# A decoder layer in float32 on one Trainium2 core: the first six projection units summed over feature blocks in six PSUM banks, their modulation fetched in matching column steps, and router logits laid out in token rows

## The chip, the core and the metric

The kernel runs on one core of a Trainium2 chip. A core has TensorE (PE; its weight loads are shown apart as PEld), VectorE (DVE), ScalarE (ACT), GpSimd (POOL), and SyncE (SP), which here only starts transfers (DMAs). The metric is device microseconds of one execution of the whole kernel. Lower is better.

## What is computed

One decoder layer for 256 tokens of width 1024, all in float32, cut to what matters here:

```python
sh1, sc1, gt1, sh2, sc2, gt2 = jnp.split(silu(c) @ w_ada + b_ada, 6)
h = rmsnorm(x, norm1) * (1.0 + sc1) + sh1                 # 256 x 1024
proj = h @ w_in                                           # q, k, v | mLSTM qk, v, o, i/f | two gates
y_a = diff_attention(q, k, v, lam)                        # 4 heads, causal, ALiBi
y_m = mlstm(silu(causal_conv(ml_qk)), ml_v, i_f)          # 4 heads
x = x + gt1 * ((sigmoid(g_a) * (y_a @ w_br_a) + sigmoid(g_m) * (y_m @ w_br_m)) @ w_out)
h2 = rmsnorm(x, norm2) * (1.0 + sc2) + sh2
x = x + gt2 * hier_moe(h2)      # 4 groups of 8 experts: best group, two experts in it, all 32 weights read
return rmsnorm(x, norm_f)
```

## The kernel before, in words

**Units.** SP streams all weights through a ring of eight slots, in units of 1 MB. The order is the list UNITS (line 54). The six 1024-column parts of `w_ada` take four units each (`ada0` to `ada5`; a unit is two of the eight feature blocks by 1024 columns). A projection unit ("dense") is all eight feature blocks by 256 columns of `w_in`. Before a unit is requested, SP waits until the job that read the same slot eight units earlier is done (line 336). SP stands in that wait with everything that is listed after it.

**Splits.** Every dense product is made of three fp32r products, so that float32 precision is kept. ACT rounds a dense unit into `hi` (`split(d)`, lines 420 to 426, one of three buffers). POOL then subtracts it from the unit, in pieces of 512 columns, and leaves the low part (line 391). PE multiplies hi by hi, low by hi and hi by low (`product`, line 1238): 24 matmuls of 256 columns for each half of a unit. The modulated input `h` is kept in the same two parts, `hT_hi` and `hT_lo`.

**Banks.** PE writes into eight PSUM banks. The list JOBS (line 94) gives every result a bank, in turn: job n uses bank n mod 8. `take(job)` makes PE wait until the job eight places earlier has been read out. `cols` and `ada2` are eight places apart, and so share a bank; DVE reads `cols` out at line 882.

**The stage around the change.** PE computes `ada0` and `ada1` (the shift and scale of the first norm) as their units land. It transposes the normalised input (`xT0` to `xT3`). DVE and ACT apply the modulation out of PSUM, and only then do the products start: `if` (the input and forget gates of the mLSTM), four q/k units `qk0` to `qk3`, `ada3`, two v units `v0` and `v1`. Then come the attention scores of all four heads (`s0` to `s7`), the units `ml0`, `ml1`, then `ada4`, `ml2`, `ml3`; then `cols` and `Mb` (decay terms of the mLSTM), `mv0`, `mv1`, `rb` (router bias) and `ada2`. Further projections, the branches and the output follow, and then the router and the MoE loop.

**Orders written by hand.** Each engine runs its instructions strictly in the order of its code. ACT has, in this order: small DMA issues, the sum of squares of x, a wait for those DMAs (`bc_in`, line 435), the modulation, splits 0 to 2, then for each of `qk0` to `qk3` a copy out of PSUM and one split, two more splits, and then for each head the exponentials, a copy of `ml{h}` and a split. DVE has the gate arithmetic (lines 777 to 806: `ifT`, then scans), `scores(h)` (lines 808 to 820), `combine(h)` (822 to 832), `conv(i)`, and then the column forms of the modulation and the copy of `cols`.

**Router and MoE.** The router logits are computed transposed (36 rows by 256 tokens, line 1486) into the bank `lgT`, copied by DVE (line 1030), transposed back by PE (line 1498) into `lg`, and read by DVE (line 1032). The MoE loop reads 96 units of expert weights. Sixteen are requested before the loop starts, into slots as they come free (lines 360 to 364); each later one waits until the loop has used up a unit (line 356, semaphore `used`).

## Time and profile before

| | |
|---|---|
| median of 3 runs | 506.74 us (506.46 to 506.91) |
| the profiled execution | 506.75 us |
| its span in the profile | 505.0 us |
| PE busy | 426.5 us (84%) |
| DVE busy | 159.5 us (32%) |
| ACT busy | 173.7 us (34%) |
| POOL busy | 157.3 us (31%) |
| data moved | 163.19 MB, mean 323 GB/s |

The profile is of one execution. Times are microseconds from the start of the span. 1.75 us of the execution lie outside the span. Busy shares are means over stages with different limits: PE is close to fully busy up to about 260 us, and from about 300 us the DMA engines are. Where an engine waited, a row names in brackets the idle time before it and what ended that.

### The profile page before, as it was taken

Reading aid. Unit: us, or ns where it says so; the run is one execution under the profiler, and the core shown is the slowest. Engines: PE = TensorE matmul, PEld = TensorE weight load, DVE = VectorE, ACT = ScalarE, POOL = GpSimd, SP = SyncE. Lnnn points to the kernel's source line nnn. Section 1 sums busy time; section 2 is a strip of 40 time slices with the busy share of each in tenths; the row PEclk is TensorE's granted clock in tenths of the full one; section 3 lists DMA queues with packets and bytes.
Section 4 is the critical chain, followed back from the end, with each engine's and each line's share of the span. In section 5 each row is a group of like instructions: output and inputs, shape, how many; then the busy total and the mean of one; then the engine's idle time right before and its main releaser. Section 6 shows DMA issues by size and latency. Waiting matters only on the chain.

```text
span 505.0 us, 8937 instructions
## 1 busy us (share of the span) xinstructions
PE 426.5 (84%) x3772; PEld 319.0 (63%) x3772; DVE 159.5 (32%) x345; ACT 173.7 (34%) x305; POOL 157.3 (31%) x126
## 2 busy tenths in 40 slices
PE   1847998999999999999987989898849668594983
PEld 0415987999899999997965636354416244261541
DVE  0243304899692430455244011202110201102014
ACT  1235431853558276533452322130301102030122
POOL 0009894765936857997400000000000000000000
PEclk9969999998999999999997999999989979799798
DMA  8999979397598437558879699999999999999942
GB/s 295 392 364 388 281 242 387 123 342 244 182 355 257 165 112 262 185 194 287 332 286 422 254 392 424 420 421 421 420 422 421 424 422 422 422 420 422 423 197 85
DMA packets 55719, 163.19 MB, mean 323 GB/s; under 512 B 7058, under 2 KB 33924, under 8 KB 43268
## 3 DMA queue, kind: packets, MB, share of 16 engines
q1 hardware_dynamic: 50528, 159.53, 82.4%
q10 hardware_dynamic: 5156, 3.17, 2.1%
q8 instruction: 25, 0.41, 0.3%
q14 instruction: 10, 0.08, 0.0%
HBM read 161.64 MB, written 1.05 MB: 322 GB/s over the span
## 4 chain that ended last, share of the span: by engine, by line
PE 62%; DMA 24%; DVE 4%; SPq 3%; ACT 2%; issue 2%; POOL 1%; DVEq 0%; ACTq 0%
PE bank L1249 33%; DMA ring<-in_w_e 15%; PE bank L1558 8%; DMA mqk<-in_w_e 5%; PE bank L1570 4%; PE bank L1531 4%; DMA ring<-in_w_ada 4%; PE bank L1520 3%; PE bank L1202 3%; SPq L351 2%; SPq L339 1%; POOL ring_r L391 1%; PE bank L1604 1%; PE bank L1486 1%; ACT ring_r L426 1%
## 5 line engine op out<-in xcount | busy, mean ns | idle before, releaser
L391 POOL TENSOR_TENSOR ring_r<-ring,ring_r 128x512 fp32r<-128x512 f32 x120 | 156.9, 1345 | 87.8 <-ACT ring_r L426 87.6
L1249 PE MATMUL bank<-ring_r 128*128 128x256 f32 x832 | 111.3, 285 | 4.6 <-DVE att L815 2.3
L1249 PEld LDWEIGHTS bank<-ring_r 128*128 128x128 f32 x832 | 103.8, 191 | 7.3 <-issue 4.3
L648 ACT ACTIVATE raw<-bank,sm 128x128 f32<-128x128 f32 x72 | 27.1, 457 | 165.1 <-PE bank L1531 165.1
L426 ACT ACTIVATE ring_r<-ring 128x2048 fp32r<-128x2048 f32 x30 | 57.4, 1912 | 43.6 <-PE bank L1249 26.1
L1558 PE MATMUL bank<-ring,raw 128*32 128x256 f32 x768 | 51.9, 423 | 17.3 <-DMA ring<-in_w_e 16.9
L1558 PEld LDWEIGHTS bank<-ring,raw 128*32 128x32 f32 x768 | 28.3, 121 | 39.5 <-issue 27.8
L1127 DVE TENSOR_TENSOR tmp<-bank,tmp 128x256 f32<-128x256 f32 x8 | 3.4, 425 | 134.0 <-ACT tmp L656 134.0
L1531 PEld LDWEIGHTS bank<-const,xn 128*128 128x128 f32 x288 | 35.9, 199 | 9.0 <-issue 7.8
L1531 PE MATMUL bank<-const,xn 128*128 128x128 f32 x288 | 37.7, 286 | 1.1 <-DVE const L1078 1.1
L1202 PE MATMUL bank<-ring,sm 128*32 128x256 f32 x384 | 27.3, 434 | 12.3 <-DMA ring<-in_w_ada 12.3
L1570 PE MATMUL bank<-ring,WT 128*32 128x512 f32 x192 | 32.3, 595 | 3.5 <-DVE WT L1132 3.5
L1249 PE MATMUL bank<-hT_r,ring_r 128*128 128x256 f32 x256 | 34.8, 279 | 0.0
L1520 PE MATMUL bank<-v,const 128*128 128x512 f32 x72 | 32.5, 593 | 1.7 <-DVE sm L1158 1.7
L1249 PEld LDWEIGHTS bank<-hT_r,ring_r 128*128 128x128 f32 x256 | 32.2, 189 | 0.0
L1202 PEld LDWEIGHTS bank<-ring,sm 128*32 128x32 f32 x384 | 12.3, 120 | 24.3 <-DMA ring<-in_w_ada 9.4
L1138 DVE TENSOR_TENSOR v<-bank,att 128x512 f32<-128x512 f32 x16 | 10.3, 685 | 42.7 <-PE bank L1570 42.7
L1570 PEld LDWEIGHTS bank<-ring,WT 128*32 128x32 f32 x192 | 8.9, 109 | 22.5 <-issue 19.6
L1520 PEld LDWEIGHTS bank<-v,const 128*128 128x128 f32 x72 | 13.0, 190 | 15.5 <-issue 15.5
L1558 PE MATMUL bank<-hT,raw 128*32 128x256 f32 x64 | 16.9, 418 | 5.5 <-DMA mqk<-in_w_e 5.5
L1249 PE MATMUL bank<-raw_r,ring_r 128*128 128x256 f32 x128 | 18.0, 282 | 0.0
L1558 PE MATMUL bank<-qkT,raw 128*32 128x256 f32 x64 | 16.9, 418 | 0.0
(301 smaller groups left out, 533.3 us busy)
## 6 DMA issues: line engine op xcount, KB each, us to landing
ring<-in_w_e SPq DMA_DIRECT2D x72, 1024.0 KB, 25.9
ring<-in_w_ada SPq DMA_DIRECT2D x24, 1024.0 KB, 10.8
ring<-in_w_in SPq DMA_DIRECT2D x22, 1024.0 KB, 8.5
hT<-in_w_e SPq DMA_DIRECT2D x6, 1024.0 KB, 23.1
qkT<-in_w_e SPq DMA_DIRECT2D x6, 1024.0 KB, 25.1
gm<-in_w_e SPq DMA_DIRECT2D x6, 1024.0 KB, 26.3
mqk<-in_w_e SPq DMA_DIRECT2D x6, 1024.0 KB, 26.2
ring<-in_w_out SPq DMA_DIRECT2D x4, 1024.0 KB, 5.1
```

The source lines that it names most:

```text
L339: sp.dma_start(unit(n, 2), w_ada[:, k0:k0 + 2, i * D:(i + 1) * D]).then_inc(landed[slot_of(n)], 16)
L351: sp.dma_start(slot(i), expert).then_inc(landed[i], 16)
L391: pool.tensor_tensor(ring_r[:, slot_of(n), sl], ring[:, slot_of(n), sl], hi(d)[:, sl].bitcast(F32), ALU.subtract).then_inc(s["w_lo"], 1)
L426: act.activation(hi(d), ring[:, slot_of(n), :], ACT.Copy).then_inc(s["w_hi"], 1)
L648: ins = act.activation(xg[:, b, k, :], token_bank[:, j * P:(j + 1) * P], ACT.Identity, bias=S("B2p", KD)[:, k:k + 1], scale=S("A2p", KD)[: ...
L1138: ins = dve.tensor_tensor(outs2[:, sl], out_banks[c][:], gt2b[:, sl], ALU.mult)
L1202: ins = pe.matmul(ps[32 * u:32 * u + 32, 0:256], S("cs", 8)[:, k:k + 1].to_broadcast([P, 32]), w[:, k - k0, 256 * u:256 * u + 256], start= ...
L1249: ins = pe.matmul(out, left(k), right(k), start=(i == 0 and k == 0), stop=(i == 2 and k == nk - 1))
L1520: ins = pe.matmul(y_banks[2 * tt + c][:], ptg[:, b, tt, :], outs2[:, 512 * c:512 * c + 512], start=False, stop=stop, skip_group_check=True)
L1531: ins = pe.matmul(token_bank[:, j * P:(j + 1) * P], xn[:, tt, k * P:(k + 1) * P], pone[:, tt].rearrange("p a n -> p (a n)"), start=(tt == ...
L1558: ins = pe.matmul(up_bank[e * CAP:(e + 1) * CAP, half], xg[:, b, k, e * CAP:(e + 1) * CAP], wt[e][:, k, :], start=(k == 0), stop=(k == KD ...
L1570: ins = pe.matmul(out_banks[c][e * CAP:(e + 1) * CAP, :], hidT[:, f, e * CAP:(e + 1) * CAP], wt[e][:, f, 512 * c:512 * c + 512], start=(f ...
```

## The change

It does three things.

**First products.** `ada0` and `ada1` are replaced by eight units of kind "mod": unit pair j holds the 256 columns of shift and the 256 columns of scale that belong to feature blocks 2j and 2j+1, over all eight input blocks. The q, k and v units are replaced by eight units of kind "block": one feature block by the first 1536 columns of `w_in` (0.75 MB). The bytes are the same. PE walks over the feature blocks: for each it adds three passes (hi by hi, hi by low, low by hi) of ten matmuls to six banks, which hold `qk0` to `v1` all that time; the remaining two banks, 6 and 7, serve the modulation steps. The v products take 512 columns at once instead of 256. A slot with a block is free when `k_done` says so.

**Orders.** `if` comes after these products. The scores of the heads are spread over `ada3`, `ml0` and `ml1`. The gate arithmetic of DVE moves in between the scores. ACT's splits and copies are put in another order, and its DMA issue of the constants comes after split 7.

**Router.** The logits are accumulated with tokens as rows (36 columns for each token half), so that the copy and the transposes fall away, and one bank job less is used.

```diff
-    units = ada(0) + ada(1)
-    units += w_in(C_Q, 2) + w_in(C_K, 2) + ada(3) + w_in(C_V, 2)
+    def mod(j):
+        return [("mod", 256 * j), ("mod", D + 256 * j)]
+
+    def block(*ks):
+        return [("block", k) for k in ks]
+
+    units = mod(0) + block(0, 1) + mod(1) + block(2, 3) + mod(2) + block(4) + mod(3) + block(5, 6, 7) + ada(3)
...
-    jobs = ["ada0"] * 4 + ["ada1"] * 4 + [f"qk{i}" for i in range(4)] + ["ada3"] * 4 + ["v0", "v1"]
+    jobs = ["sa0"] * 2 + ["k0", "k1"] + ["sa1"] * 2 + ["k2", "k3"] + ["sa2"] * 2 + ["k4"] + ["sa3"] * 2
+    jobs += ["k5", "k6", "k7"] + ["ada3"] * 4
...
-JOBS = (["cT", "ada0", "vT"] + [f"xT{i}" for i in range(4)] + ["adaT0", "ada1", "adaT1", "if"]
-        + ["qk0", "ifT", "qk1", "qk2", "qk3"]
-        + ["ada3", "v0", "adaT3", "v1"] + [f"s{i}" for i in range(8)] + ["ml0", "ml1", "ada4", "ml2", "ml3", "adaT4"]
+FIRST_JOBS = ([("cT", 6), ("vT", 7)] + [(f"xT{i}", i) for i in range(4)] + [("sa0", 6), ("sT0", 7)]
+              + [(f"qk{i}", i) for i in range(4)] + [("v0", 4), ("v1", 5)]
+              + [("sa1", 6), ("sT1", 7), ("sa2", 6), ("sT2", 7), ("sa3", 6), ("sT3", 7)])
+JOBS = (["if", "s0", "s1", "ada3", "ifT", "s2", "s3", "adaT3", "ml0", "s4", "s5", "ml1", "s6", "s7", "ada4", "ml2", "ml3",
+         "adaT4"]
...
+        def spent(n):
+
+            kind, k = UNITS[n]
+            if kind == "block":
+                return (s["k_done"], k + 1) if k < KD - 1 else full("v1")
+            return full(UNIT_JOB[n])
...
-                    sp.wait_ge(*full(UNIT_JOB[n - RING]))
+                    sp.wait_ge(*spent(n - RING))
+                if kind == "mod":
+                    sp.dma_start(unit(n, 8), w_ada[:, :, c0:c0 + 256]).then_inc(landed[slot_of(n)], 16)
+                    continue
+                if kind == "block":
+                    sp.dma_start(slot(slot_of(n))[:, 0:FIRST], w_in[:, c0, 0:FIRST]).then_inc(landed[slot_of(n)], 16)
+                    continue
...
+            for i in range(2):
+                act.wait_ge(*full(f"xT{i}"))
+                release(act.activation(hT[:, 2 * i:2 * i + 2, :], pb(f"xT{i}")[:].rearrange("p (a n) -> p a n", a=2),
+                                       ACT.Copy), f"xT{i}")
+
+            def modulate_hi(j):
+
+                act.wait_ge(*free(f"xT{j}"))
+                act.wait_ge(s["mod1"], j + 1)
+                for k in (2 * j, 2 * j + 1):
+                    act.activation(hT_hi[:, k, :], hT[:, k, :], ACT.Identity, bias=S("m1", 16)[:, k:k + 1],
+                                   scale=S("A1", KD)[:, k:k + 1]).then_inc(s["h_hi"], 1)
+
+            split(0)
+            modulate_hi(0)
+            split(1)
+            for j in range(1, 4):
+                split(2 * j)
+                if j < 3:
+                    split(2 * j + 1)
+                modulate_hi(j)
+            split(7)
...
+            split(8)
+            split(9)
             for i in range(4):
                 act.wait_ge(*full(f"qk{i}"))
                 release(act.activation(qkT[:, 2 * i:2 * i + 2, :], pb(f"qk{i}")[:].rearrange("p (a n) -> p a n", a=2),
                                        ACT.Copy), f"qk{i}")
-                split(3 + i)
-                if i == 1:
-                    act.wait_ge(s["gates"], 2)
-                    act.activation(grow[0:4, 2, :], grow[0:4, 2, :], ACT.Exp).then_inc(s["gexp"], 1)
-                    act.wait_ge(s["gexp"], 1)
-                    act.activation(grow[0:4, 2, :], grow[0:4, 2, :], ACT.Ln, bias=1.0).then_inc(s["gln"], 1)
-            split(7)
-            split(8)
+            split(10)
...
-                split(9 + h)
+                split(11 + h)
+                if h == 0:
+                    act.wait_ge(s["gates"], 2)
+                    act.activation(grow[0:4, 2, :], grow[0:4, 2, :], ACT.Exp).then_inc(s["gexp"], 1)
+                    act.wait_ge(s["gexp"], 1)
+                    act.activation(grow[0:4, 2, :], grow[0:4, 2, :], ACT.Ln, bias=1.0).then_inc(s["gln"], 1)
...
+            def mod_rows(j):
+
+                dve.wait_ge(*full(f"sa{j}"))
+                if j >= 2:
+                    dve.wait_ge(*full(f"sT{j - 2}"))
+                release(dve.tensor_copy(arow[:, j % 2, 0:P], pb(f"sa{j}")[:, 0:P]), f"sa{j}")
...
+
+                two = slice(2 * j, 2 * j + 2)
+                dve.wait_ge(*full(f"sT{j}"))
+                turned = pb(f"sT{j}")[:, 0:P].rearrange("p (a i r) -> p a i r", a=2, i=2)[:, :, :, 0]
+                release(dve.tensor_tensor(m1.rearrange("p (a k) -> p a k", a=2)[:, :, two], turned,
+                                          col("b_ada", 0, 16).rearrange("p (a k) -> p a k", a=2)[:, :, two], ALU.add),
+                        f"sT{j}")
+                dve.wait_ge(*free(f"sT{j}"))
+                own(dve.scalar_tensor_tensor(out=S("A1", KD)[:, two], in0=m1[:, 8 + 2 * j:10 + 2 * j], scalar=1.0,
+                                             in1=col("norm1", 2 * j, 2), op0=ALU.add, op1=ALU.mult), "mod1", j + 1)
+                dve.wait_ge(*free(f"xT{j}"))
+                for i in range(2):
+                    k = 2 * j + i
+                    ins = dve.tensor_scalar(tmp[:, 1, i * T:(i + 1) * T], hT[:, k, :], S("A1", KD)[:, k:k + 1],
+                                            m1[:, k:k + 1], ALU.mult, ALU.add)
+                link(ins)
+                for i in range(2):
+                    k = 2 * j + i
+                    dve.wait_ge(s["h_hi"], k + 1)
+                    dve.tensor_tensor(hT_lo[:, k, :], tmp[:, 1, i * T:(i + 1) * T], hT_hi[:, k, :].bitcast(F32),
...
                 ins.then_inc(s["conv_out"], 1)
 
             scores(0)
+            rows(3)
+            gate_inputs()
             scores(1)
+            columns(B2, 3)
+            dve.tensor_copy(S("B2_r", KD), B2).then_inc(s["mod2"], 1)
             combine(0)
             scores(2)
             combine(1)
...
+            def mod_rows(j):
+
+                ps = take(f"sa{j}")
+                w = []
+                for c0 in (256 * j, D + 256 * j):
+                    n = landing[("mod", c0)]
+                    pe.wait_ge(landed[slot_of(n)], landed_value(n))
+                    w.append(unit(n, 8))
+                for k in range(KD):
+                    for u in range(4):
+                        ins = pe.matmul(ps[32 * u:32 * u + 32, 0:P], S("cs", 8)[:, k:k + 1].to_broadcast([P, 32]),
+                                        w[u // 2][:, k, (u % 2) * P:(u % 2 + 1) * P], start=(k == 0), stop=(k == KD - 1),
+                                        tile_position=(0, 32 * u))
+                filled(ins, f"sa{j}")
...
+            def first_pass(k, w, h, start, stop):
+
+                for i in range(8):
+                    ins = pe.matmul(pb(f"qk{i // 2}")[:, (i % 2) * T:(i % 2 + 1) * T], w[:, i * P:(i + 1) * P], h,
+                                    start=start and i % 2 == 0, stop=stop, skip_group_check=True)
+                    if stop and i % 2:
+                        filled(ins, f"qk{i // 2}")
+                for tt in range(TT):
+                    ins = pe.matmul(pb(f"v{tt}")[:], h[:, tt * P:(tt + 1) * P], w[:, 1024:FIRST], start=start, stop=stop,
+                                    skip_group_check=True)
+                    if stop:
+                        filled(ins, f"v{tt}")
+                return ins
+
+            mod_rows(0)
+            mod_turn(0)
+            for job in first_jobs:
+                take(job)
+            for k in range(KD):
+                assert UNITS[DENSE[k]] == ("block", k)
+                w_hi, w_lo = hi(k)[:, 0:FIRST], ring_r[:, slot_of(DENSE[k]), 0:FIRST]
+                pe.wait_ge(s["w_hi"], k + 1)
+                pe.wait_ge(s["h_hi"], k + 1)
+                first_pass(k, w_hi, hT_hi[:, k, :], k == 0, False)
+                if k % 2 and k < 7:
+                    mod_turn(k // 2 + 1)
+                pe.wait_ge(s["h_lo"], k + 1)
+                first_pass(k, w_hi, hT_lo[:, k, :], False, False)
+                pe.wait_ge(s["w_lo"], lows(k))
+                ins = first_pass(k, w_lo, hT_hi[:, k, :], False, k == KD - 1)
+                if k < 7:
+                    ins.then_inc(s["k_done"], 1)
+                if k % 2 == 0 and k < 6:
+                    mod_rows(k // 2 + 1)
+            at[0], dense[0] = DENSE[KD - 1] + 1, KD
...
-                if i == 2:
-                    ada(4)
-                proj_T(f"ml{i}", hsrc, next_dense(8))
+
+            scores(0)
+            ada(3)
+            ps = take("ifT")
+            pe.wait_ge(*free("if"))
+            for g in range(2):
+                ins = pe.matmul(ps[0:4, g * T:(g + 1) * T], ident[0:8, 4 * g:4 * g + 4], grow[0:8, 2, :],
+                                start=True, stop=True)
+            filled(ins, "ifT")
+            scores(1)
+            ada_turn(3)
+            proj_T("ml0", hsrc, next_dense(8))
+            scores(2)
+            proj_T("ml1", hsrc, next_dense(8))
+            scores(3)
+            ada(4)
+            proj_T("ml2", hsrc, next_dense(8))
+            proj_T("ml3", hsrc, next_dense(8))
...
             def logits(ks):
                 for k in ks:
-                    ins = pe.matmul(pl[0:G + NE, 0:T], w_r[:, k, :], hT[:, k, :], start=(k == 0), stop=(k == KD - 1))
+                    for tt in range(TT):
+                        ins = pe.matmul(pl[:, tt * 36:(tt + 1) * 36], hT[:, k, tt * P:(tt + 1) * P], w_r[:, k, :],
+                                        start=(k == 0 and tt == 0), stop=(k == KD - 1), skip_group_check=True)
                 return ins
...
             pe.wait_ge(*free("x2T3"))
-            filled(logits((6, 7)), "lgT")
-            ps = take("lg")
-            pe.wait_ge(*free("lgT"))
-            for tt in range(TT):
-                ins = pe.transpose(ps[:, tt * 36:(tt + 1) * 36], lgT[0:G + NE, tt * P:(tt + 1) * P],
-                                   ident[0:G + NE, 0:G + NE])
-            filled(ins, "lg")
```

On ACT, from the first copy of q and k to the first exponentials, before (names: `ring_r` at line 426 is a split, `qkT` a copy of `qk` results, `o` at line 470 the gate rows):

```order
L465 ACTIVATE qkT<-bank 128x512
L426 ACTIVATE ring_r<-ring 128x2048
L465 ACTIVATE qkT<-bank 128x512
L426 ACTIVATE ring_r<-ring 128x2048
L470 ACTIVATE o<-o 4x256
L472 ACT_TABLE_LOAD
L472 ACTIVATE o<-o 4x256
...
L426 ACTIVATE ring_r<-ring 128x2048 x3
L479 ACT_TABLE_LOAD
L479 ACTIVATE att,sm<-att,sm 128x128
```

The same stretch of ACT after the change, from the splits ahead of the copies on:

```order
L453 ACTIVATE ring_r<-ring 128x2048 x2
L500 ACTIVATE qkT<-bank 128x512 x4
L453 ACTIVATE ring_r<-ring 128x2048
L507 ACTIVATE att,sm<-att,sm 128x128
L510 ACTIVATE att,sm<-att,sm 128x256
L507 ACTIVATE att,sm<-att,sm 128x128
L510 ACTIVATE att,sm<-att,sm 128x256
L516 ACTIVATE raw<-bank 128x2x256
L453 ACTIVATE ring_r<-ring 128x2048
L521 ACTIVATE o<-o 4x256
L523 ACT_TABLE_LOAD
```

The four copies now stand behind two splits, those of `ml0` and `ml1` (splits 8 and 9). The gate rows stand behind the exponentials of head 0.

On PE after the change, from the last pass of the block loop to the first pass of `ml0` (L1295 is a product with the gate weights, then `ml0`; L1408 and L1409 are scores, L1248 is `ada3`, L1417 is `ifT`):

```order
L1295 MATMUL bank<-hT_r,w_if_hi 8x256 x8
L1408 MATMUL bank<-qkT 128x128
L1409 MATMUL bank<-qkT 128x256
L1408 MATMUL bank<-qkT 128x128
L1409 MATMUL bank<-qkT 128x256
L1248 MATMUL bank<-ring,sm 32x256 x32
L1417 MATMUL bank<-o,const 4x256 x2
L1408 MATMUL bank<-qkT 128x128
L1409 MATMUL bank<-qkT 128x256
L1408 MATMUL bank<-qkT 128x128
L1409 MATMUL bank<-qkT 128x256
L1258 MATMUL bank<-const,arow 128x128 x2
```

Before, `ada3` stood ahead of `v0`, and the scores of all heads followed `v1`. Now `ada3` stands behind the scores of head 0, which read `qkT`.

## Rows read from the trace of the kernel before

**Rows 1.** Stretches of the span: length, busy of PE, PEld, DVE, ACT, POOL; PEclk, DMA share, GB/s
```profile
34.00:35.00 1.00, 0.00 (x0) 0.00 (x0) 1.00 (x3) 1.00 (x3) 0.00 (x0) 0.50 1.11 349
...
282.00:284.00 2.00, 2.00 (x37) 1.24 (x30) 0.00 (x0) 0.00 (x0) 0.00 (x0) 1.00 0.00 0
...
300.00:320.00 20.00, 17.91 (x194) 10.45 (x184) 3.35 (x8) 4.67 (x10) 0.00 (x0) 1.00 1.01 423
```

**Rows 2.** The chain that ended last: start, length, engine and line
```profile
50.70 17.17 PE bank L1249 x144
...
88.41 11.56 PE bank L1249 x96
...
131.23 1.71 PE bank L1376 x16
132.94 3.59 PE bank L1202 x64
```

**Rows 3.** Timeline of ACT, 13 to 31 us
```profile
13.70 1.06 ACT L431 ACTIVATE hT<-x 128x1024 f32<-128x1024 f32 x1 [7.74 <-issue]
...
30.05 0.26 ACT L436 ACTIVATE w_if_hi<-w_if 128x64 fp32r<-128x64 f32 x1 [12.64 <-DMA tmp<-in_lam_k]
```

**Rows 4.** DMA queues (packets, MB, share) from 8 to 26 us, then 54 to 55 us
```profile
q1 hardware_dynamic: 1772, 6.80, 96.9%
q10 hardware_dynamic: 1775, 0.13, 6.8%
...
q1 hardware_dynamic: 272, 0.31, 97.2%
q10 hardware_dynamic: 274, 0.00, 20.8%
```

**Rows 5.** Timeline of PE, 10 to 25 us
```profile
10.14 1.94 PE L1202 MATMUL bank<-ring,sm 128*32 128x256 f32 x16 [6.49 <-DMA ring<-in_w_ada]
...
20.09 3.21 PE L1286 MATMUL bank<-const,xn 128*128 128x128 f32 x16
...
23.45 1.93 PE L1202 MATMUL bank<-ring,sm 128*32 128x256 f32 x32
```

**Rows 6.** One DMA group, 60 to 71 us: transfers, size, us from issue to landing
```profile
ring<-in_w_in SPq DMA_DIRECT2D x2, 1024.0 KB, 5.2
```

**Rows 7.** Timeline of ACT, 67 to 94 us
```profile
67.91 0.60 ACT L465 ACTIVATE qkT<-bank 128x512 f32<-128x512 f32 x1 [2.14 <-PE bank L1249]
...
88.84 1.92 ACT L426 ACTIVATE ring_r<-ring 128x2048 fp32r<-128x2048 f32 x1 [9.52 <-DMA ring<-in_w_in]
90.77 1.28 ACT L479 ACT_TABLE_LOAD   x1
...
93.75 0.19 ACT L482 ACTIVATION_READ_ACCUMULATOR att<-att,sm 128x1 f32 x1
```

**Rows 8.** Timeline of DVE, 85 to 130 us
```profile
85.07 0.41 DVE L800 TENSOR_TENSOR o<-o 4x256 f32<-4x256 f32 x1
...
87.39 0.41 DVE L805 SCALAR_TENSOR_TENSOR o<-o 4x256 f32<-4x256 f32 x1
...
93.97 0.18 DVE L825 RECIPROCAL sm<-sm 128x4 f32<-128x4 f32 x1 [1.72 <-ACT att L482]
...
99.41 0.17 DVE L825 RECIPROCAL sm<-sm 128x4 f32<-128x4 f32 x1
...
129.72 0.16 DVE L882 COPY sm<-bank 128x16 f32<-128x16 f32 x1
```

**Rows 9.** The router: timeline of PE, then of DVE, 260 to 264 us
```profile
260.83 1.05 PE L1486 MATMUL bank<-hT,w_r 128*36 128x256 f32 x4 [0.69 <-ACT hT L612]
...
262.88 0.23 DVE L1032 TENSOR_TENSOR router<-bank,sm 128x72 f32<-128x72 f32 x1 [0.47 <-PE bank L1498]
```

**Rows 10.** PE ahead of the MoE loop, and the stretch behind its wait (columns of rows 1)
```profile
267.29 0.38 PE L1509 MATMUL bank<-router,const 128*128 128x32 f32 x2 [2.53 <-DVE router L1068]
...
269.00:270.00 1.00, 0.59 (x3) 0.59 (x3) 0.97 (x3) 0.00 (x0) 0.00 (x0) 0.50 0.99 418
```

More of the change, by code:

```diff
@@ L81 @@
 NPRE = len(UNITS)
-DENSE = [n for n, (kind, _) in enumerate(UNITS) if kind != "ada"]
+DENSE = [n for n, (kind, _) in enumerate(UNITS) if kind not in ("ada", "mod")]
+WIDTH = [FIRST if UNITS[n][0] == "block" else UNIT for n in DENSE]
 QUAD_UNITS = [(w, e) for w in ("w1", "w3", "w2") for e in range(QUAD)]
@@ L388, in _ @@
                 pool.wait_ge(s["w_hi"], d + 1)
-                for part in range(PARTS):
-                    sl = slice(part * UNIT // PARTS, (part + 1) * UNIT // PARTS)
+                for c in range(0, WIDTH[d], PART):
+                    sl = slice(c, c + PART)
                     pool.tensor_tensor(ring_r[:, slot_of(n), sl], ring[:, slot_of(n), sl], hi(d)[:, sl].bitcast(F32),
@@ L519, in _ @@
             copy_a(2)
-            split(15)
+            split(17)
             copy_a(3)
@@ L588, in _ @@
                 release(ins, f"ymT{i}")
-            for d in range(25, 28):
+            for d in range(27, 30):
                 split(d)
@@ L778, in _ @@
             release(dve.tensor_scalar(grow[0:8, 2, :], pb("if")[0:8, 0:T], S("b_if", 1)[0:8, :], None, ALU.add), "if")
-            dve.wait_ge(*full("ifT"))
-            release(dve.tensor_copy(grow[0:4, 0:2, :], pb("ifT")[0:4, :].rearrange("p (a n) -> p a n", a=2)), "ifT")
-            dve.wait_ge(*free("ifT"))
-            link(dve.tensor_scalar(grow[0:4, 3, :], grow[0:4, 1, :], -1.0, None, ALU.mult))
-            own(dve.tensor_tensor(grow[0:4, 2, :], grow[0:4, 3, :], grow[0:4, 1, :], ALU.min), "gates", 1)
@@ L785, in _ @@
-            own(dve.tensor_scalar(grow[0:4, 3, :], grow[0:4, 1, :], 0.0, None, ALU.min), "gates", 2)
-            B2, A2 = S("B2", KD), S("A2", KD)
-            rows(3)
-            for i in range(2):
-                dve.wait_ge(*full(f"v{i}"))
-                if i == 1:
-                    columns(B2, 3)
-                    dve.tensor_copy(S("B2_r", KD), B2).then_inc(s["mod2"], 1)
-                release(dve.tensor_copy(v[:, :, 256 * i:256 * i + 256],
-                                        pb(f"v{i}")[:].rearrange("p (t n) -> p t n", t=2)), f"v{i}")
@@ new lines, in _, with gate_inputs @@
+            B2, A2 = S("B2", KD), S("A2", KD)
+            def gate_inputs():
+                dve.wait_ge(*full("ifT"))
+                release(dve.tensor_copy(grow[0:4, 0:2, :], pb("ifT")[0:4, :].rearrange("p (a n) -> p a n", a=2)), "ifT")
+                dve.wait_ge(*free("ifT"))
+                link(dve.tensor_scalar(grow[0:4, 3, :], grow[0:4, 1, :], -1.0, None, ALU.mult))
+                own(dve.tensor_tensor(grow[0:4, 2, :], grow[0:4, 3, :], grow[0:4, 1, :], ALU.min), "gates", 1)
+                own(dve.tensor_scalar(grow[0:4, 3, :], grow[0:4, 1, :], 0.0, None, ALU.min), "gates", 2)
@@ L1287, in _ @@
                 filled(ins, f"xT{i}")
-            ada_turn(0)
-            ada(1)
-            ada_turn(1)
+            pe.wait_ge(*free("cT"))
+            landing = {u: n for n, u in enumerate(UNITS)}
+            def mod_rows(j):
[11 more added lines that the diff above has]
+                filled(ins, f"sa{j}")
@@ new lines, in mod_turn @@
+            def mod_turn(j):
+                ps = take(f"sT{j}")
+                pe.wait_ge(*free(f"sa{j}"))
+                filled(pe.transpose(ps[:, 0:P], arow[:, j % 2, 0:P], ident), f"sT{j}")
+            first_jobs = [f"qk{i}" for i in range(4)] + ["v0", "v1"]
+            def first_pass(k, w, h, start, stop):
[10 more added lines that the diff above has]
+                return ins
@@ L1299, in _, with scores @@
             for i in range(4):
-                if i == 1:
-                    ps = take("ifT")
-                    pe.wait_ge(*free("if"))
-                    for g in range(2):
-                        ins = pe.matmul(ps[0:4, g * T:(g + 1) * T], ident[0:8, 4 * g:4 * g + 4], grow[0:8, 2, :],
-                                        start=True, stop=True)
-                    filled(ins, "ifT")
-                proj_T(f"qk{i}", hsrc, next_dense(8))
-            ada(3)
-            proj("v0", hsrc, next_dense(8))
-            ada_turn(3)
-            proj("v1", hsrc, next_dense(8))
-            for i in range(4):
                 pe.wait_ge(*free(f"qk{i}"))
-            for h in range(HEADS):
+            def scores(h):
                 for c in range(2):
```

146 lines of the change are left out of this document (58 added, 88 removed).

## The prediction

> **What bounds the kernel now.** I read the stretches first, from the end backwards. From 300 us on the DMA engines are busy all the time at 423 GB/s, while at 282 to 284 us they stand still: the sixteen expert units requested ahead have landed, and the next waits until the MoE loop has used one up [rows 1]. So the end of the kernel is the start of that loop plus a constant, and what the loop's start gains or loses goes through to the end whole. Then the chain of waits: from 50.70 us it is one PE piece after another up to the router (q/k units, `ml0` and `ml1` from 88.41, `rb`, `ada2` at 132.94) [rows 2]. In that stage PE is the bound, with DVE close behind: DVE finishes the copy of `cols` at 129.9 [rows 8], and `ada2` needs that bank. DVE is thus only 3.1 us ahead of PE there, and it works without a pause from 93.97 to 129.9 (35.9 us). That is the place to watch. `ada2` started at 132.94; its new start is what I work out. The profiled execution took 506.75 us and the median of the runs is 506.74, so the sum can be read against either. About 0.2% (1 us) is what a measurement of this kernel can tell from no change.
>
> **Start of the first block.** Before, ACT could begin the sum of squares only at 13.70, after 7.74 us of DMA issues [rows 3]: its queue is full of small packets. While two queues have work they alternate one packet for one (1772 to 1775 over 18 us, with big packets on SP's queue; 272 to 274 in one microsecond, with 1 KB packets there) [rows 4]. The new first units have 1 KB packets, so ACT's small ones drain 2.7 times as fast: 272 per us against 98. I take ACT free at 10.2 (bounds: 9.5 and the old 13.7) and the small loads landed at about 19 instead of 30.05 [rows 3]. From ACT's start to the transposes of x it was 6.4 us (13.70 to 20.09), of which PE was kept by `ada0` for about one: 10.2 + 5.5 = 15.7, transposes 3.2 [rows 5] to 18.9. Then the first modulation step on PE. The same instruction took 1.94 us for 16 records at 10.14 and 1.93 us for 32 at 23.45 [rows 5]: PE begins at 1.2 GHz. A step has 64 such records of half the columns; slow, that is 3.5 us (between 1.8 and 6.9), to 22.4. Turning it into columns and applying it is a copy, a transpose and three short steps, about 1.9: the first block starts at 24.3.
>
> **The block loop.** A pass has ten matmuls, together the work of twelve of 256 columns, each 0.119 us (144 in 17.17) [rows 2]: 1.4 us, 4.2 for a block, 33.6 for eight. The products themselves cost the same as before; the wider v matmuls may save 0.1 us a pass. POOL's subtraction is 3 pieces a block instead of 4 and stays beside it. Three modulation steps lie between the blocks: columns halved but as many instructions as `ada2`'s 3.59 [rows 2], so between 1.8 and 3.6; I take 2.4, in all 7.2. The Trainium skill (TensorE: Matmul & The Clock Gate, "Wait — 56ns, not 53.3ns?") gives a floor of about 25 ns from start to start; by it 64 records would be 1.6 us, and the sum 2.4 us less.
> The loop is also held by its own requests. Units of `mod` 3 are requested when block 1 is done, at 24.3 + 4.2 + 2.4 + 4.2 = 35.1. A lone 1 MB unit lands in 5.2 us [rows 6], of which 3.0 are transfer at 349 GB/s [rows 1]. Two mod units and block 5 (0.75 MB, 2.1 us at 378 GB/s, the 6.80 MB of [rows 4]) then land at 35.1 + 2.2 + 3.0 + 3.0 + 2.1 = 45.4. ACT applies the modulation of block 4 only behind the split of block 5 (three quarters of 1.92 [rows 7], and 0.6): block 4 starts at 47.5 where PE is ready at 45.9. The loop ends at 24.3 + 33.6 + 7.2 + 1.6 = **66.7**. Before, `ml0` began at 88.41 [rows 2], behind the same products, `if`, `ada3` and all scores.
>
> **Where it goes again: ACT's order.** The copies of q and k stand behind splits 8 and 9, so they wait for the landing of `ml1`. Behind block 5 the queue has two blocks (4.2), four units of `ada3` (11.2), `ml0` and `ml1` (6.0), and 1.4 MB of constants and router weights (3.9), whose issue now falls here: 45.4 + 25.3 = 70.7. Split 1.9, four copies at 0.6, which overlap a little, 2.2 [rows 7]: 74.8. PE meanwhile does `if` (2.8) to 69.5 and waits 5.3. Scores of head 0 (0.9, an estimate: four short float32 matmuls) and `ada3` (3.6) end at 79.3. Only then are the units behind `ada3` requested: two of `ada4` and `ml2` land 2.2 + 5.6 + 3.0 = 10.8 later, 90.1. ACT's split 10 stands ahead of the exponentials of head 0: with 1.9, and 1.9 for these (88.84 to 93.94 [rows 7] less split and table load, which is not needed now), 93.9. `combine(0)` starts there, as before (93.97).
>
> **DVE's chain becomes the bound.** From there DVE has its 35.9 us, plus the gate sums, which were done ahead of it (85.07 to 87.80, 2.7) [rows 8]. And `combine(1)` waits: ACT puts a copy 0.5, a split 1.9, the gates 2.1 (a table load 1.3 and two short steps at 0.4), another table load 1.3 and the exponentials 1.9 ahead, 7.7 in all, where DVE is ready after 5.4 (93.97 to 99.41): 2.3 more. 93.9 + 35.9 + 2.7 + 2.3 = 134.8, so `ada2` starts at about 134.9: **+2.0** against 132.94. PE would be there some 5 us earlier and waits.
>
> **The clock.** PE now waits about 5 us ahead of head 0's scores and again ahead of `ada2`. A wait of 2.53 us was followed by half the granted clock two microseconds later, with PE busy again [rows 10]. `ada3` or `ada2` at 1.2 GHz takes 3.6 us more. I take one such fall or two halves: **+3.0** (bounds 0 and 7.2). The Trainium skill's page on TensorE ("What's actually happening") says that the slow clock is the default and activity releases it; it speaks against this change, and by it both falls would come, +7.2 in place of +3.0.
>
> **The router.** The tail was 1.05 us of matmuls, a DVE copy and two transposes, 260.83 to 262.88 [rows 9]. Now four matmuls of 36 columns at 0.21 (1.71 for eight [rows 2]): DVE reads at 261.8. **-1.1**. The input of the loop that ACT scales is not later, so it goes through.
>
> Sum: 2.0 + 3.0 - 1.1 = +3.9, **510.7 us**.
>
> **The rivals.** *The copies do not wait* (faster). If `ml1` lands by 65.4 instead of 70.7, splits 8 and 9 are done before `if` ends at 69.5. `ada3` then ends at 74.0, all that follows comes 5.3 us earlier, DVE's chain still bounds `ada2` (129.6), the long wait of PE at the scores is gone and with it the fall: -3.3 - 1.1 = -4.4, **502.3**; with modulation steps at 1.8 us and an early start it reaches 498. For it: only 5 us are needed, and each us that the first two blocks gain lets SP ask for the third pair as much earlier. Against: the bytes ahead of `ml1` are fixed.
> *ACT still waits for the small loads until 30.05* (much slower). Then split 0 ends at 33.0 and POOL's low part at 37.0, where the forecast's third pass starts at 27.1: +9.9 on everything, **520**. For it: the wait was 12.64 us long [rows 3]. Against: the count of packets. The Trainium skill (DMA: Bandwidth & Descriptors, "Queues, rings and completion order") lets each engine alternate between its queues by packets, which agrees with [rows 4].
> *Nothing moves:* DVE's chain holds `ada2` at 133 to 134.5, no fall of the clock: 506 to 507.5.
>
> **How the numbers follow.** Forecast (507.8 to 516) 0.54, copies free (495 to 505.7) 0.27, nothing 0.08, small loads (516 and more) 0.11. Forecast and small loads give slower: 0.65. The range 499 to 518 takes in the free copies but for their lower end, and the forecast with both clock falls; it leaves about 0.2 outside.
>
> **What would show it.** In the new profile: ACT's first split at 20 to 22 (right) or after 30 (small loads); the last matmul of the block loop near 67; the first q/k copy behind a split that waited for a DMA of `w_in`; PE idle some 5 us ahead of the first scores; `ada2` waiting for DVE's copy of `cols`, near 135; DVE's first `combine` near 94. The prediction is wrong if `ada2` waits for nothing, or if the first `combine` comes before 90.

## The result: 515.69 us, slower by 1.55%

| | before | changed |
|---|---|---|
| median | 506.83 us (506.46 to 508.95, 4 runs) | 515.69 us (513.36 to 516.69, 4 runs) |
| ratio | | 1.0155, 95% interval 1.0127 to 1.0182 |
| profiled execution / span | 506.75 / 505.0 us | 515.02 / 513.2 us |
| PE / DVE / ACT busy | 426.5 / 159.5 / 173.7 us | 434.1 / 170.0 / 175.0 us |

The forecast was 510.7 (499 to 518), slower with a chance of 0.65. Sign and range held; the loss, 8.9 us, was more than twice the 3.9 forecast. The changed kernel was run and profiled once more, beside its variants: 514.41 us. That profile is the "second profile" below (an execution of 513.26 us).

The profile of the changed kernel, timeline of PE (start, length, engine, line; in brackets the idle time before and what ended it):

```profile
17.65 3.15 PE L1346 MATMUL bank<-ring,sm 128*32 128x128 f32 x64
22.86 1.48 PE L1362 MATMUL bank<-ring_r 128*128 128x256 f32 x8 [1.25 <-ACT ring_r L475]
...
50.41 1.66 PE L1362 MATMUL bank<-ring_r 128*128 128x256 f32 x8 [2.29 <-ACT ring_r L475]
...
71.05 1.08 PE L1295 MATMUL bank<-ring_r,w_if_hi 128*8 128x256 f32 x8
...
80.33 0.81 PE L1408 MATMUL bank<-qkT 64*128 64x128 f32 x4 [6.34 <-ACT qkT L500]
80.89 1.10 PE L1409 MATMUL bank<-qkT 64*128 64x256 f32 x4
81.91 5.16 PE L1248 MATMUL bank<-ring,sm 128*32 128x256 f32 x64
...
123.56 0.66 PE L1258 MATMUL bank<-const,arow 128*128 128x128 f32 x2 [5.96 <-DVE arow L737]
124.14 0.58 PE L1436 MATMUL bank<-const,o 4*128 4x4 f32 x4
124.59 3.75 PE L1443 MATMUL bank<-o,const 4*128 4x256 f32 x8
...
144.22 3.66 PE L1248 MATMUL bank<-ring,sm 128*32 128x256 f32 x64
```

The gain is real and is lost again within 10 us. The products of q, k and v end at 71.05, with `if` (2.8 us), the scores of head 0 and `ada3` (3.66 at the full clock) still to do; without a wait all of that would be done near 78.4 (an estimate from these rows). Before, PE had done the products, `if` and `ada3` when it came to the first scores, at 83.10:

```profile
83.10 0.50 PE L1320 MATMUL bank<-qkT 64*128 64x128 f32 x4
```

But now PE waits 6.34 us for the q/k copies and runs `ada3` in 5.16 us, to 87.0, and waits 5.96 us more at 123.56. `ada2` starts at 144.22, 11.3 us later than before.

Its timeline of ACT: two splits that each wait for a landing, the copies behind them, and the next split 18 us later, with the exponentials of head 0 behind it (answers to [rows 3, 7]):

```profile
8.63 1.06 ACT L458 ACTIVATE hT<-x 128x1024 f32<-128x1024 f32 x1 [2.69 <-issue]
...
19.28 0.26 ACT L463 ACTIVATE w_if_hi<-w_if 128x64 fp32r<-128x64 f32 x1 [6.95 <-DMA tmp<-in_lam_k]
...
72.50 1.92 ACT L453 ACTIVATE ring_r<-ring 128x2048 fp32r<-128x2048 f32 x1 [3.62 <-DMA ring<-in_w_in]
76.21 1.91 ACT L453 ACTIVATE ring_r<-ring 128x2048 fp32r<-128x2048 f32 x1 [1.80 <-DMA ring<-in_w_in]
78.03 2.04 ACT L500 ACTIVATE qkT<-bank 128x512 f32<-128x512 f32 x4
98.23 1.91 ACT L453 ACTIVATE ring_r<-ring 128x2048 fp32r<-128x2048 f32 x1 [18.16 <-DMA ring<-in_w_in]
```

Its timeline of DVE, 101 to 144 us (answers to [rows 8]): the first `combine`, the five gate sums, the copy of `ada4`'s rows on which PE waited, and the copy of `cols`:

```profile
101.93 0.18 DVE L869 RECIPROCAL sm<-sm 128x4 f32<-128x4 f32 x1 [9.49 <-ACT att L510]
...
113.25 1.51 DVE L844 TENSOR_TENSOR o<-o 4x256 f32<-4x256 f32 x1
114.80 1.67 DVE L846 TENSOR_TENSOR_SCAN o<-const,o 4x256 f32<-4x256 f32 x1
116.50 1.34 DVE L847 TENSOR_TENSOR o<-o 4x256 f32<-4x256 f32 x1
117.88 1.63 DVE L848 TENSOR_TENSOR_SCAN o<-const,o 4x256 f32<-4x256 f32 x1
119.55 1.31 DVE L849 SCALAR_TENSOR_TENSOR o<-o 4x256 f32<-4x256 f32 x1
...
122.99 0.41 DVE L737 COPY arow<-bank 128x256 f32<-128x256 f32 x1
...
143.06 0.16 DVE L931 COPY sm<-bank 128x16 f32<-128x16 f32 x1
```

The gate sums take 7.5 us. Before they took 2.7 [rows 8], in a stretch in which POOL did nothing; now POOL is at work from 111.75 to 123.20. The copy of `cols` comes at 143.06, 1.2 us before `ada2`, which needs that bank: both chains arrive nearly together. In this profile `ada2` itself waits for nothing; the wait for DVE is the one at 123.56, for the copy of `ada4`'s rows.

Of these 11.3 us, 8.2 reach the end. The router gave back 0.7: DVE reads the logits 1.36 us after the start of the last logit matmuls, before it was 2.05. The start of the MoE loop gave back 1.2, since it ran more at the full clock: its first wide products (L1604, now L1702) take 1.88 us instead of 3.05. From the loop's first products with a weight unit to the end it is 223.7 us, before it was 224.8. There the stop of the DMA engines [rows 1] is shorter: before, they were busy for 0.24 of the six microseconds from 280, now for 0.29 of the three from 291, so they stood still for 4.6 and 2.1 us. (Length, busy shares, PEclk, DMA share, GB/s; of before, then of the changed kernel.)

```profile
280.00:286.00 6.00, 5.76 (x81) 4.47 (x82) 1.07 (x3) 0.74 (x2) 0.00 (x0) 1.00 0.24 68
```

```profile
291.00:294.00 3.00, 3.00 (x51) 2.16 (x41) 0.00 (x0) 0.00 (x0) 0.00 (x0) 1.00 0.29 115
```

### The profile page after: what moved, and what is told of

Read it like the earlier page. It is cut to its first block, busy times and chain, and to the rows that moved or that the text cites. A ratio compares the mean times of both kernels' runs of the same rounds, so it can differ in the third digit from the quotient of the medians.

```text
span 513.2 us, 9163 instructions
## 1 busy us (share of the span) xinstructions
PE 434.1 (85%) x3866; PEld 327.4 (64%) x3866; DVE 170.0 (33%) x358; ACT 175.0 (34%) x309; POOL 156.9 (31%) x126
## 4 chain that ended last, share of the span: by engine, by line
PE 59%; DMA 21%; DVE 9%; issue 3%; ACT 3%; SPq 2%; ACTq 1%; DVEq 0%
PE bank L1295 21%; DMA ring<-in_w_e 15%; PE bank L1656 9%; DMA ring<-in_w_in 6%; PE bank L1668 6%; PE bank L1629 5%; PE bank L1618 4%; PE bank L1362 3%; PE bank L1248 2%; SPq L378 2%; PE bank L1346 1%; PE bank L1367 1%; DVE xn L874 1%; PE bank L1589 1%; PE bank L1330 1%
## 5 line engine op out<-in xcount | busy, mean ns | idle before, releaser
L1295 PE MATMUL bank<-ring_r 128*128 128x256 f32 x640 | 86.1, 286 | 0.7 <-ACT ring_r L627 0.7
L1295 PEld LDWEIGHTS bank<-ring_r 128*128 128x128 f32 x640 | 80.5, 193 | 2.6 <-issue 1.4
L453 ACT ACTIVATE ring_r<-ring 128x2048 fp32r<-128x2048 f32 (+1 forms) x32 | 57.6, 1801 | 57.3 <-DMA ring<-in_w_in 34.3
L1668 PE MATMUL bank<-ring,WT 128*32 128x512 f32 x192 | 37.0, 648 | 3.8 <-DVE WT L1179 3.8
L1295 PE MATMUL bank<-hT_r,ring_r 128*128 128x256 f32 x192 | 26.1, 279 | 0.0
L1295 PEld LDWEIGHTS bank<-hT_r,ring_r 128*128 128x128 f32 x192 | 24.2, 189 | 0.0
L1362 PE MATMUL bank<-ring_r 128*128 128x256 f32 x128 | 19.6, 299 | 3.5 <-ACT ring_r L475 3.5
L1362 PEld LDWEIGHTS bank<-ring_r 128*128 128x128 f32 x128 | 18.3, 203 | 5.8 <-ACT ring_r L453 2.9
L1295 PE MATMUL bank<-raw_r,ring_r 128*128 128x256 f32 x128 | 18.0, 282 | 0.0
## 6 DMA issues: line engine op xcount, KB each, us to landing
gm<-in_w_e SPq DMA_DIRECT2D x6, 1024.0 KB, 24.3
```

The source lines that it names most:

```text
L453: act.activation(hi(d)[:, 0:WIDTH[d]], ring[:, slot_of(n), 0:WIDTH[d]], ACT.Copy).then_inc(s["w_hi"], 1)
L1295: ins = pe.matmul(out, left(k), right(k), start=(i == 0 and k == 0), stop=(i == 2 and k == nk - 1))
L1362: ins = pe.matmul(pb(f"qk{i // 2}")[:, (i % 2) * T:(i % 2 + 1) * T], w[:, i * P:(i + 1) * P], h, start=start and i % 2 == 0, stop=stop, sk ...
L1668: ins = pe.matmul(out_banks[c][e * CAP:(e + 1) * CAP, :], hidT[:, f, e * CAP:(e + 1) * CAP], wt[e][:, f, 512 * c:512 * c + 512], start=(f ...
```

## The experiments

Theory A: ACT's order (copies behind the splits of units still on their way), and behind it DVE's chain, cost the time. Rivals: the supply of units; the half clock behind the waits.

### The q/k copies ahead of splits 8 and 9

```diff
-            split(8)
-            split(9)
             for i in range(4):
                 act.wait_ge(*full(f"qk{i}"))
                 ...
+            split(8)
+            split(9)
             split(10)
```

> Theory A (the order on ACT costs the time): the q/k copies run at 71 to 73.5 instead of 78.0 to 80.1, scores of head 0 start near 74 instead of 80.3, the half clock there goes, ada3 ends near 79 instead of 87.1, ml2 lands 8 us earlier and all behind it follows: 507 to 509 us. Theory B (supply: the units come no earlier than they do, whatever ACT's order): scores start at 74, but the stage behind ml2 does not move and the time stays within 2 us of the changed kernel (513 to 517).

505.42 us, ratio to before 0.9948 (0.9911 to 0.9984). Two lines moved turn the loss into a small gain.

> The changed kernel itself, unaltered, beside the runs that follow. If its block loop is as in the variants (if products start at 66.5 to 67.5 instead of 71.0), the whole is 3 to 4 us shorter than first measured: 511.5 to 513.5 us, a ratio of 1.009 to 1.012. If the first measurement holds: 514 to 517, 1.014 to 1.018.

514.41 us, ratio 1.0161 (1.0132 to 1.019). The first measurement holds. Its profile has the `if` products at 66.81, not 71.05: the late block loop of the first profile was that execution's, and is not the loss. It began with block 0: two DVE instructions of the first modulation step took 2.62 us there, beside POOL's first subtraction, and 0.74 in the second profile, where they ran ahead of it. PE then waited 0.95 us and ran at half the clock, and the next step began 2.6 us later (31.06 against 28.49).

> copies_first once more, on the same chip as the changed kernel. Theory A: the scores of head 0 start near 69.5 to 71 instead of 76 to 80, all behind follows: 6 to 9 us less than changed_again.

505.64 us on the same chip, ratio 0.9974 (0.9954 to 0.9995): 8.8 us less than the changed kernel beside it. Its timeline of PE:

```profile
70.30 0.50 PE L1408 MATMUL bank<-qkT 64*128 64x128 f32 x4
70.62 0.61 PE L1409 MATMUL bank<-qkT 64*128 64x256 f32 x4
...
113.48 0.66 PE L1258 MATMUL bank<-const,arow 128*128 128x128 f32 x2 [7.61 <-DVE arow L737]
```

The scores follow the `if` products at once, and all units behind `ada3` are requested 8 us earlier: it was not the supply. PE still waits 7.6 us for DVE at `ada4`'s rows.

### Split 10 behind the exponentials of head 0

```diff
-            split(10)
...
+                if h == 0:
+                    split(10)
+
                 act.wait_ge(s["pads"], 1)
```

> Only the split of ml2 is moved, behind the exponentials of head 0. Theory A: the scores still start at 80.3, but combine(0) starts near 87 instead of 101.9. ACT then reaches the exponentials of head 1 only 2 us earlier, since the split of ml2 still waits for its landing at 98: combine(1) near 108 instead of 110.4, PE waits 3 to 4 us for the rows of ada4 instead of 6: 511 to 513 us. Rival (DVE's chain as a whole is the bound): combine(0) was its start, so 8 us and more come off, 505 to 507.

511.31 us, ratio 1.0081 (1.0051 to 1.0111). The time is Theory A's, and DVE's chain is not held by `combine(0)` alone: that starts at 89.05, but `combine(1)` only at 105.2 (expected near 108), PE still waits 5.18 us at the rows of `ada4` (expected 3 to 4), and `ada2` starts at 140.21, 0.3 us earlier than in the second profile.

> Both moves together. Theory A: scores of head 0 at 74, ada3 ends at 79, combine(0) near 80, ml2 lands at 90; exponentials of head 1 end near 100 and DVE's gate sums are done near 111; PE is ready for the rows of ada4 at 109.5, waits 2 to 4 us, and ada2 starts at 133 to 135 instead of 144.2: 504 to 507 us, no slower than before the change. Theory B (supply): over 511.

505.32 us, ratio 0.994 (0.9905 to 0.9974): the same as the copies alone. `combine(0)` now runs at 83, but `combine(1)` at 98.5, as in copies_first (98.65): ACT's exponentials of head 1 stand behind two more splits and the gate rows, and PE waits 6.45 us, not 2 to 4. My reading that DVE's chain starts with `combine(0)` was too simple; ACT feeds it head by head.

### The gate sums early

On ACT: copies, splits 8 and 9, exponentials of head 0, gate rows, exponentials of head 1, split 10. On DVE:

```diff
+            gate_sums()
             combine(0)
             scores(2)
             combine(1)
-            gate_sums()
             scores(3)
             rows(4)
```

> The changed kernel with ACT in the order: q/k copies, splits 8 and 9, exponentials of head 0, gate rows, exponentials of head 1, split 10; and DVE's gate sums ahead of combine(0). Theory A (in the changed kernel PE waits for DVE's copy of ada4's rows, which stands behind gate sums that take 7.5 us beside POOL instead of 2.7): the gate sums fall where POOL stands still (83 to 90), take about 2.7 us, DVE is done with its part before PE, the wait of 6 us ahead of the rows' transpose and the half clock behind it are gone, ada2 starts at 122 to 125: 494 to 498 us. Rival (the supply of units bounds PE next): PE waits for ml2 or ml3, and the time stays over 501 us.

506.94 us, ratio 0.9987 (0.9967 to 1.0007): no gain over the copies alone (505.42). The first half of the expectation held: the gate sums took 2.65 us (82.20 to 84.85, POOL idle), and PE ran without a wait to 123. Then:

```profile
132.13 5.31 PE L1258 MATMUL bank<-ring,sm 128*32 128x256 f32 x64 [9.15 <-DVE sm L941]
```

This is the wait of the forecast: `ada2` for DVE's copy of `cols`. DVE's work had been moved forward, and into the time in which POOL is at work. Its timeline, 97 to 109 us:

```profile
97.33 1.22 DVE L892 TENSOR_SCALAR mqk<-raw,cols 128x256 f32<-128x256 f32 x1
98.58 4.28 DVE L895 SCALAR_TENSOR_TENSOR mqk<-raw,cols,mqk 128x256 f32<-128x256 f32 x3
102.90 1.27 DVE L892 TENSOR_SCALAR mqk<-raw,cols 128x256 f32<-128x256 f32 x1
104.20 4.21 DVE L895 SCALAR_TENSOR_TENSOR mqk<-raw,cols,mqk 128x256 f32<-128x256 f32 x3
```

Three such instructions of a convolution took 1.53 us in the changed kernel where POOL stood still; here they take 4.2.

### Which of DVE's results PE waits for

```diff
             combine(1)
+            rows(4)
             gate_sums()
             scores(3)
-            rows(4)
```

> The changed kernel with DVE's copy of ada4's rows directly behind combine(1), ahead of the gate sums and the scores of head 3. Theory A: the transpose of these rows follows ml3 without a wait, and PE waits at the next step, cols, for the gate sums that end at 121: the wait of 6.0 us becomes one of 3 to 4 us, the half clock stays: 512 to 514 us. If the copy's place alone made the wait, 8 us come off: 507.

521.83 us, ratio 1.0276 (1.0249 to 1.0304): slower than either forecast, and than the changed kernel. The wait did move to `cols` and shrank to 3.42 us, as expected, but a second one appeared behind it, 8.65 us at `ada2`, with half the clock after it. DVE began `combine(0)` 2.0 us earlier there than in the changed kernel (99.90 against 101.93), but reached the copy of `cols` 3.5 us later (146.56 against 143.06). The 5.5 us between lie from `combine(2)` on, where `conv(1)` and `combine(3)` fell beside POOL. Timelines of POOL and DVE, of this run and then of the changed kernel:

```profile
132.63 5.49 POOL L418 TENSOR_TENSOR ring_r<-ring,ring_r 128x512 fp32r<-128x512 f32 x4 [3.02 <-ACT ring_r L453]
134.16 4.24 DVE L885 SCALAR_TENSOR_TENSOR mqk<-raw,cols,mqk 128x256 f32<-128x256 f32 x3
```

```profile
135.50 1.53 DVE L885 SCALAR_TENSOR_TENSOR mqk<-raw,cols,mqk 128x256 f32<-128x256 f32 x3
138.78 5.57 POOL L418 TENSOR_TENSOR ring_r<-ring,ring_r 128x512 fp32r<-128x512 f32 x4 [6.99 <-ACT ring_r L453]
```

Next, the copy of `cols` and the four decay arguments, which free the banks of `ada2`, `o0` and `o1`, ahead of `combine(3)`, `conv(1)` and the own columns:

```diff
+            dve.wait_ge(*full("cols"))
+            release(dve.tensor_copy(S("ccol", 16), pb("cols")[:, 0:16]), "cols")
+            for h in range(HEADS):
+                decay_arg(h)
+            combine(3)
             conv(1)
-            combine(3)
...
-            dve.wait_ge(*full("cols"))
-            release(dve.tensor_copy(S("ccol", 16), pb("cols")[:, 0:16]), "cols")
```

> rows4_first (521.8 us, ada2 waited 8.65 us for DVE's copy of cols and then ran at half the clock, 5.8 us) with that move added. Theory A: both go, and 9 to 11 us come off: 511 to 513 us. Rival: PE waits for another result of DVE at the same time, and the time stays over 518.

515.47 us, ratio 1.0169 (1.0132 to 1.0207): 6.4 us less than rows4_first, between the two forecasts. `ada2` starts at 137.63 instead of 146.78, without a wait; 3.96 us go back to the next late bank, the router bias, at 160.08.

> The changed kernel with that move on DVE alone. There PE waits at the rows of ada4 and ada2 did not wait for cols, so Theory A has nothing to gain: 514 to 517 us. If the shared bank cost something all the same, 508 to 512.

512.8 us, ratio 1.0104 (1.0073 to 1.0136), 1 to 3 us less than the changed kernel, between the two ranges. In the second profile `ada2` did wait 0.57 us for `cols`: the chains are nearly tied.

> As gates_early, and on DVE the copy of cols and the four decay arguments stand ahead of combine(3), conv(1) and the own columns. Theory A (in gates_early ada2 waited 9.15 us for DVE's copy of cols, since they share a bank and DVE's chain runs beside POOL at a third of its speed): the copy falls near 112.5, PE starts ada2 near 123 without a wait and with the full clock (3.7 instead of 5.3 us): 495 to 498 us. Rival (DVE as a whole is the bound): PE soon waits for the q/k terms of the mLSTM or the rows of ada2 instead, and the time stays over 502.

500.05 us, ratio 0.9847 (0.9819 to 0.9876), 7.7 us faster than before. Its timeline of PE:

```profile
104.85 0.38 PE L1268 MATMUL bank<-const,arow 128*128 128x128 f32 x2
...
122.81 3.66 PE L1258 MATMUL bank<-ring,sm 128*32 128x256 f32 x64
...
144.62 2.87 PE L1305 MATMUL bank<-ring_r 128*128 128x256 f32 x16 [3.33 <-DVE rbias L963]
```

The waits at `ada4`'s rows and at `cols` are gone and `ada2` starts 10.1 us earlier than before. The time is 2 us over the expectation, since a new wait stands at 144.62.

> As cols_early, and DVE adds the router bias, which frees the bank of rb for the first gate unit, ahead of conv(2) and conv(3). Theory A (the next late release of a bank by DVE, seen in cols_early as a wait of 3.33 us with half the clock for some 2 us behind it): the wait and the half clock go, 3.5 to 5 us come off: 495 to 497 us, a ratio of 0.975 to 0.98. Rival (PE now waits for the q/k terms of the mLSTM, which these two convolutions finish): 499 to 501.

499.28 us (six runs, 496.04 to 505.32; without the longest 498.93), ratio 0.9829 (0.979 to 0.9869). That wait is gone, and one of 2.78 us at 154.84 takes its place. The time lies in the rival's range, but not by its mechanism: PE waits for the bank of `o0`, which DVE frees when it scales `o` (line 973), and DVE had waited 5.76 us there for ACT's squares of `o`. The step isn't resolved from cols_early.

### The clock

```diff
+            def fill(job, n):
+
+                ps = take(job)
+                for i in range(n):
+                    pe.matmul(ps[:, 0:P], ident, ident, start=True, stop=True)
+
+            fill("s0", 50)
             for i in range(4):
                 pe.wait_ge(*free(f"qk{i}"))
...
+            fill("adaT4", 48)
             ada_turn(4)
```

> The changed kernel with 50 matmuls without use while PE waits for the q/k copies and 48 while it waits for the rows of ada4, each 0.11 us. If the waits of 6.3 and 6.0 us cost nothing but their length, the time stays within 1 us of the changed kernel. If the half clock that follows each of them is an extra cost (ada3 took 5.2 instead of 3.7 us, the products with the gate rows 3.75 instead of 1.97), the granted clock stays at 1.0 and 4 to 5 us come off: 510 to 511.5 us.

516.2 us, ratio 1.0188 (1.0142 to 1.0234). It tells little: the fills took 11.32 and 10.88 us, nearly twice the waits. But `ada3` ran in 3.66 us, the gate products in 1.97, and from the transpose of `ada4`'s rows to `ada2` PE took 16.4 us instead of 20.9. So `ada2` started at 143.62, only 3.1 us later than in the second profile, whose block loop ended alike.

> As the kernel with the filled waits, but half as many fills, 27 and 25: each is two records, and the fills took 11.3 and 10.9 us where the waits were 6.3 and 6.0. Now they take 6.1 and 5.7. If the half clock is an extra cost beside the waits: 4 to 5 us less than the changed kernel, 510 to 512 us, ada3 in 3.7 us and the gate products in 2.0. If it is none: 514 to 517.

521.41 us, ratio 1.0277 (1.0245 to 1.031). `ada3` took 3.66 us again, and the time rose: PE came to `ada2` 0.7 us sooner than in the second profile and waited 4.93 us there for `cols`. DVE was level with the second profile up to `combine(3)` (133.14 against 133.06) and then reached the copy of `cols` 3.7 us later (143.98 against 140.31), beside a subtraction of POOL that began at 133.84 instead of 134.52.

> cols_only (512.8 us) with 27 and 25 fills of PE's two waits, which last 6.1 and 5.7 us where the waits were 6.6 and 6.1. Behind the first wait ada3 took 5.98 us instead of 3.66, behind the second the gate products 3.76 instead of 1.97 and the next products half the clock for 6 us more. If the half clock is an extra cost: ada3 in 3.7, no half clock behind the second wait, 509 to 511 us. If the waits that follow are DVE's, they grow by what the clock gives, and it stays at 512 to 513.5.

With `cols` out of the way: 513.89 us, ratio 1.0141 (1.0112 to 1.0169), against 1.0104 for cols_only. Nothing gained. Its profile is of the longest of the seven executions, 518.86 us. The first fill ended 2.13 us early and `ada3` ran in 5.35 us all the same; behind the second PE came to `ada2` at 139.05 (141.23 in cols_only) and gave it back in a wait of 3.35 us for the router bias, which DVE reached 4.6 us later than in cols_only (160.54 against 155.99). In none of the three did the time fall, since DVE's results were late or became later. None prices the clock by itself: the fills also shifted when DVE and POOL meet.

### The router alone

The kernel before with the last hunks of the change.

> The kernel before with the router part of the change alone. The forecast's step: DVE reads the logits 1.1 us earlier and the loop starts 1.1 us earlier: 505.5 to 506.0 us, a ratio of 0.998. Rival: the 32 matmuls of 36 columns instead of 8 of 256 keep the last step as long as before, and nothing changes.

506.94 us, ratio 0.9977 (0.9961 to 0.9994), or 1.2 us: the forecast's size, but not shown at the forecast's place. Its profile, at half the clock there (1.92 us for the last matmuls), has DVE read 2.02 us after their start, no less than before (2.05). In the changed kernel's first profile it is 1.36 us, in the second 2.03.

## Why the prediction was right in its sign and wrong in its size

| step | forecast | first profile | second profile |
|---|---|---|---|
| ACT free | 10.2 | 8.63 | 8.48 |
| small loads landed | 19 | 19.28 | 19.58 |
| first block | 24.3 | 22.86 | 22.82 |
| end of the block loop | 66.7 | 71.05 | 66.81 |
| `ml1` landed | 70.7 | 76.21 | 72.84 |
| `ada3` ends | 79.3 | 87.0 | 83.0 |
| `ml2` landed | 90.1 | 98.23 | 94.38 |
| `combine(0)` | 93.9 | 101.93 | 98.08 |
| DVE's copy of `cols` | 134.8 | 143.06 | 140.31 |
| `ada2` | 134.9 | 144.22 | 140.53 |
| execution | 510.7 | 515.02 | 513.26 |

**The mechanism held up to DVE's chain.** The copies wait for a landing, the units behind `ada3` are asked for late, split 10 holds the exponentials, and DVE's chain arrives with `ada2`. The runs show it: moving the copies alone takes 8.8 us off. The rival "copies do not wait" fell by the landing of `ml1` at 72.84 and 76.21, where it needed 65.4; "small loads" fell at 19.28. The end of the block loop, 66.81 for 66.7, is partly luck: the first block came 1.5 us early, and the loop took 44.0 us instead of 42.4, though its modulation steps took 1.95 us each and not 2.4.

One of my own signs of being wrong came true: in the first profile `ada2` waits for nothing, and in the second for 0.57 us, where I had PE wait about 5.

**What was mis-sized is the term +2.0 for `ada2`,** which measured +7.6 in the second profile (+11.3 in the first), in four pieces. The landing of `ml1` came 2.1 us later than summed. Scores and `ada3` took 6.1 us instead of 4.5, since much of both ran below the full clock behind the wait: I had priced that clock, but as a sum of its own. `ml2` landed 11.4 us after `ada3` instead of 10.8. From `combine(0)` to the copy of `cols` DVE needed 42.2 us, forecast 40.9. That last one is close by luck: the gate sums cost 7.5 us and not 2.7, as I had priced them from a stretch in which POOL did nothing, while the wait of 2.3 us at `combine(1)` didn't occur and the rest of the chain took about 1 us less.

**The clock term, +3.0, was put in the wrong place and too large.** In front of `ada3` the slower clock is a part of the delay of `ada2`: 0.7 us of the scores and 0.8 of `ada3` in the second profile, so 1.5 of the +7.6. Behind the second wait (gate products in 3.75 us instead of 1.97) PE's way to `ada2` is 2.7 us longer than before in the first profile, but it lies beside DVE's chain: DVE's copy of `cols` was done at 143.22, so at most 1.0 us could be had there, and nothing in the second profile, where `ada2` waited for that copy.

**The router term, -1.1, isn't shown where I put it.** From `ada2` to the end, the second profile needs 372.7 us and before needed 373.8, which is the -1.1, and +7.6 - 1.1 would have made the sum 513.2. But DVE read the logits there no sooner than before (2.03 us against 2.05); what came back came in the MoE loop. The first profile needs 370.8.

**The end is not the loop's start plus a constant.** From the first matmuls of the MoE loop to the end of the span it is 235.6 us before (from 269.41), 233.3 in the first profile (from 279.87) and 233.8 in the second (from 277.72). So about 2 us of the delay did not go through, by the clock at the loop's start and the shorter stop of the DMA engines. That works against the error above.

**The place of the waits.** I expected one ahead of `ada2`. It stood some 20 us and nine bank jobs earlier, at the transpose of `ada4`'s rows, whose copy stands behind gate sums and scores on DVE. I had listed the gate sums as a length, and not asked who waits for what is queued behind them. By clock_filled_short, rows4_first and gates_early, taking that wait away or shortening it brings out the one at `cols`.

## What to carry to other kernels

When a stage gets shorter, read each in-order queue behind it for work that waits for something later than its neighbour: here two splits of units in flight stood ahead of copies that had been ready, and two lines were worth 8.8 us. A result of a slow engine that frees a bank should be taken out before long work that nobody waits for, and work that is moved forward can land beside an engine that slows it. A length read where the neighbour engine stood still (gate sums, 2.7 us) is not its length beside that engine (7.5). Price a slower clock on the path it lies on, not as a sum of its own.
